# One decode-and-prefill layer on one core: all key products on VectorE, and the memory scan moved in front of the convolution

## What is computed

```python
h = rms_norm(x, norm1_w)
z = h @ w_in                       # conv b, c, x; q; k; v; memory q; three gates
y_conv = (zb * short_conv(zc * zx)) @ w_conv_out
q = partial_rope(rms_norm(q, q_norm_w)); k = partial_rope(rms_norm(k, k_norm_w))
# prompt: causal attention over its own 256 tokens
# sample b: over 2048 past tokens (16 pages of 128 rows) and its own
k_past = cache_k[page_table]       # per sample 16 pages, (128, 8 heads * 2 * 64)
s = einsum(q, k) * 64 ** -0.5      # differential attention: softmax 1 - lam * softmax 2
# prompt: memory keys and values from mem_prompt @ w_mem_kv, normed
# sample b: from cache_mem_k, cache_mem_v (256 tokens, 4 heads * 256)
qm = rms_norm(mq, mq_norm_w); s = einsum(qm, mem_k) * 256 ** -0.5
x = x + (sum_b sigmoid(gate_b) * y_b) @ w_o
x = x + peer_ffn(rms_norm(x, norm2_w))   # 8 heads, top 16 of 16384 experts per token
```

## Time and profile before

| | |
|---|---|
| profiled execution | 2749.54 us, span 2747.8 us |
| median of 3 runs | 2750.61 us (2749.42 to 2750.76) |
| TensorE busy | 2443.3 us (89%) |
| VectorE busy | 1431.9 us (52%) |
| ScalarE busy | 352.9 us (13%) |
| GpSimd busy | 1055.8 us (38%) |
| moved by DMA | 919.33 MB, mean 335 GB/s |
| key page scan (VectorE) | 116.24 to 485.8 us |
| memory projection (TensorE) | 446.96 to 575.4 us |
| gates and branches (TensorE) | 581.83 to about 1228 us |

### The profile page before, as it was taken

How to read it: one execution, slowest core, us unless ns; L and a number is a source line. 1 busy time by engine, 2 the same in 40 slices (tenths; PEclk the granted TensorE clock), 3 DMA queues, 4 the chain that set the end, 5 groups by cost and what they waited for, 6 DMA issues and landing times.

```text
span 2747.8 us, 27652 instructions
## 1 busy us (share of the span) xinstructions
PE 2443.3 (89%) x9109; PEld 1570.1 (57%) x9109; DVE 1431.9 (52%) x2306; ACT 352.9 (13%) x781; POOL 1055.8 (38%) x953
## 2 busy tenths in 40 slices
PE   9999998899999999999997777777999597777777
PEld 7888887778766678888884233332434142332333
DVE  3465566972322323002378877884554556554543
ACT  2111000012222211001112101111011011111110
POOL 1265566110222200000056555754544464445542
PEclk9999999999999999999999999998999899999999
DMA  7698999593799965447498999999999999999998
GB/s 225 225 343 311 323 345 333 203 343 123 280 353 352 355 215 187 159 149 235 138 369 344 422 418 417 416 418 422 422 413 422 412 408 418 419 421 418 416 421 370
DMA packets 305904, 919.33 MB, mean 335 GB/s; under 512 B 15738, under 2 KB 196050, under 8 KB 236756
## 3 DMA queue, kind: packets, MB, share of 16 engines
q0 software_dynamic: 122448, 725.64, 65.7%
q1 hardware_dynamic: 183332, 192.20, 21.4%
HBM read 909.08 MB, written 8.72 MB: 334 GB/s over the span
## 4 chain that ended last, share of the span: by engine, by line
PE 36%; DMA 24%; issue 13%; POOL 13%; DVE 11%; POOLq 2%; ACT 0%; DVEq 0%; SPq 0%; ACTq 0%
DMA sb_bregion<-in_peer_u_dram,sb_ring 14%; PE ps L788 13%; PE ps L800 6%; PE ps L694 4%; PE ps L1037 4%; DMA sb_mkv<-in_peer_u_dram,sb_ring 4%; DVE sb_bregion L1988 3%; POOL sb_ring L450 3%; POOL sb_mkv L450 3%; PE ps L888 2%; DMA sb_S<-in_peer_u_dram,sb_ring 2%; PE ps L778 2%; POOLq L441 2%; POOL sb_bregion L566 2%; POOL sb_wring L566 2%
## 5 line engine op out<-in xcount | busy, mean ns | idle before, releaser
L1037 PE MATMUL ps<-sb_wring,sb_ring 128*128 128x512 f32 x992 | 455.1, 608 | 86.7 <-DMA sb_wring<-in_peer_v_dram,sb_ring 86.6
L694 PE MATMUL ps<-sb_hT,sb_wring 128*128 128x264 f32 x1792 | 407.7, 388 | 3.4 <-DMA sb_wring<-in_w_in_dram 1.9
L1988 DVE CUSTOM_DVE_ANT_0 sb_bregion<-sb_bregion,sb_rows 128x2048 f32<-128x2048 f32 x128 | 293.5, 2293 | 217.2 <-DMA sb_bregion<-in_peer_u_dram,sb_ring 209.9
L1037 PEld LDWEIGHTS ps<-sb_wring,sb_ring 128*128 128x128 f32 x992 | 186.2, 194 | 354.4 <-issue 271.2
L694 PEld LDWEIGHTS ps<-sb_hT,sb_wring 128*128 128x128 f32 x1792 | 339.6, 191 | 62.2 <-issue 3.3
L788 PE MATMUL ps<-sb_hT,sb_wring 128*128 128x264 f32 x1536 | 368.2, 391 | 6.6 <-DMA sb_wring<-in_w_in_dram 5.1
L788 PEld LDWEIGHTS ps<-sb_hT,sb_wring 128*128 128x128 f32 x1536 | 289.2, 191 | 70.5 <-issue 16.4
L1037 PE MATMUL ps<-sb_oreg,sb_ring 128*128 128x512 f32 x496 | 236.1, 626 | 74.4 <-DMA sb_oreg<-in_peer_v_dram,sb_ring 52.0
L1037 PE MATMUL ps<-sb_hT,sb_ring 128*128 128x512 f32 x496 | 231.6, 614 | 53.6 <-DMA sb_hT<-in_peer_v_dram,sb_ring 47.5
L566 POOL DMA_INDIRECT sb_bregion<-in_peer_u_dram,sb_ring x132 | 185.7, 1407 | 226.1 <-DVEq L1376 194.5
L1037 PEld LDWEIGHTS ps<-sb_oreg,sb_ring 128*128 128x128 f32 x496 | 96.1, 200 | 213.5 <-issue 144.9
(11 more groups left out here) (376 smaller groups left out, 2785.1 us busy)
## 6 DMA issues: line engine op xcount, KB each, us to landing
sb_wring<-in_w_in_dram SPq DMA_DIRECT2D x52, 2048.0 KB, 13.0
sb_ring<-in_cache_k_dram POOLq DMA_DIRECT2D x64, 512.0 KB, 6.8
sb_mkv<-in_cache_k_dram POOLq DMA_DIRECT2D x64, 512.0 KB, 6.7
sb_mkv<-in_cache_v_dram POOLq DMA_DIRECT2D x48, 512.0 KB, 7.1
sb_rows<-in_cache_v_dram POOLq DMA_DIRECT2D x47, 512.0 KB, 7.2
sb_wring<-in_w_mem_kv_dram SPq DMA_DIRECT2D x8, 2048.0 KB, 11.7
sb_wring<-in_w_o_dram SPq DMA_DIRECT2D x8, 2048.0 KB, 8.1
sb_S<-in_cache_v_dram POOLq DMA_DIRECT2D x22, 512.0 KB, 6.8
```

Of the source, the lines that this page charges most:

```text
L694: last = mm(ps[:, (2 * r + c) % 4, 0:NT], wring[:, r, k, c * P:(c + 1) * P], rhs[:, k, :], start=(k == 0), stop=(k == KC - 1))
L1037: last = mm(ps[:, 4 * t + q, :], diag[:, k % 4, :], e_slots[v % ER][:, q * 512:(q + 1) * 512], start=False, stop=q_stop, skip_group_check= ...
L1988: st(V.tensor_tensor_reduce(out=u_slots[n % UR], in0=u_slots[n % UR], in1=h2, scale=1.0, scalar=0.0, op0=ALU.mult, op1=ALU.add, accum_out= ...
```

## The change

- `multiply_pages` and `kprod_ready` go. GpSimd only loads pages in the scan, in a loop of four turns with 8 groups each. VectorE multiplies all four pages of a group itself, into two product places in turn, and frees a page as soon as its product is made.
- The memory scan moves from behind the memory key norm to right behind the norms of the key and query rows. Its pages use the eight places of the key pages (`MEM_PAIR` picks pairs; tokens 0 and 1 use the four in `mkv` and are loaded before the norms, tokens 2 and 3 those in `ring4` after them), and each later pair is loaded two tokens ahead.
- ScalarE's memory copies wait for the end of the memory scan (2 + 16). `root(4)` moves in front of the last four convolution copies. The wait of ScalarE at the third gate chunk goes, as does GpSimd's wait for `sqrt_in`.
- The copy of the convolution state and the own maxima follow the memory key norm directly.
- The weights' blocks stay at 256 columns.

```diff
-        mem_pages = [ring4[:, n, :] for n in range(4)] + [conv_y[:, n * DC:(n + 1) * DC] for n in range(2)]
-        MEM_PAIR = [0, 1, 2, 0, 1, 2, 1, 2]
+        MEM_PAIR = [2, 3, 0, 1] * 2
...
-            load_pages(0, 0)
-            with st.loop(TS // 2 - 1, 16) as i:
+            with pool.Fori(0, TS // 2) as i:
                 for g in range(8):
-                    load_pages(i, g + 1)
-                    multiply_pages(i, g)
-            for g in range(8):
-                if g < 7:
-                    load_pages(TS // 2 - 1, g + 1)
-                multiply_pages(TS // 2 - 1, g)
+                    load_pages(i, g)
...
+            pool.wait_ge(s["kpage_used"], 8 + TS * PAGES)
+            load_memory(0)
+            load_memory(1)
             pool.wait_ge(s["q_ready"], 2)
             pool.dma_start(mq_dram, rows[0:TS, 2, 3 * DC:4 * DC]).then_inc(s["q_scratch"], 16)
             pool.wait_ge(s["q_scratch"], 32)
...
+            load_query(0)
+            load_query(1)
+            load_memory(2)
+            load_memory(3)
...
-            pool.wait_ge(s["sqrt_in"], 5)
-            load_memory(2)
             for b in range(2, TS):
                 pool.wait_ge(s["token_done"], 2 + TS + (b - 2) + 1)
                 load_query(b)
-                if b < 5:
-                    load_memory(b + 1)
-                elif b > 5:
-                    load_memory(b)
+                if b + 2 < TS:
+                    load_memory(b + 2)
...
-            conv_chunks(0, 6)
-
-            act.wait_ge(s["token_done"], 2 + TS)
+            conv_chunks(0, 5)
+            root(4, small[:, 3, 0:60])
+            conv_chunks(5, 1)
+
+            act.wait_ge(s["token_done"], 2 + 2 * TS)
...
-            root(4, small[:, 3, 0:60])
...
-                if q == 2:
-                    act.wait_ge(s["token_done"], 2 + TS + 4)
...
+                for r in range(4):
+                    dve.wait_ge(k_landed[4 * half + r], landed)
+                    if r >= 2:
+                        st.reach(k0 + r + 1)
+                    elif g:
+                        st.reach(k0 + r - 1)
+                    st.run(TT(prods[r % 2], slots[r], qb[:, par, :], ALU.mult))
+                    if r % 2:
+                        for p in (r - 1, r):
+                            st.reach(k0 + 2 * (r - 1) + p % 2 + 1)
+                            signal("kpage_used")
+                            st.run(RED(out(p), by_head(prods[p % 2]), X, ALU.add))
...
             signal("q_ready")
 
+            def score_memory(b):
...
+            for b in range(TS):
+                score_memory(b)
 
             dve.wait_ge(s["chunk_taken"], C_MEM + 4)
...
-            for b in range(TS):
-                score_memory(b)
-                if b == 4:
-                    dve.wait_ge(s["cs_full"], 1)
-                    st(CP(cs_rows[0:2 + TS, :].rearrange("p (a b) -> p a b", a=2), ps[0:2 + TS, 6:8, :]))
-                    signal("cs_rows")
-                if b == 5:
-                    own_maxima()
+            dve.wait_ge(s["cs_full"], 1)
+            st(CP(cs_rows[0:2 + TS, :].rearrange("p (a b) -> p a b", a=2), ps[0:2 + TS, 6:8, :]))
+            signal("cs_rows")
+            own_maxima()
```

More of the change, by code:

```diff
@@ L130, in build @@
         ring_flat = ring4[:, :, :].rearrange("p a b -> p (a b)")
-        conv_y = conv[:, 2 * BC:3 * BC, :].rearrange("p a b -> p (a b)")
-        mem_pages = [ring4[:, n, :] for n in range(4)] + [conv_y[:, n * DC:(n + 1) * DC] for n in range(2)]
-        MEM_PAIR = [0, 1, 2, 0, 1, 2, 1, 2]
+        MEM_PAIR = [2, 3, 0, 1] * 2
         scores = cflat[:, 0:3 * 2 * PH * NKEY].rearrange("p (t n) -> p t n", t=3)
@@ L209, in build @@
         names = """consts x_in x_in1 x_in2 x_factors x_clear xT_scaled mem_in cols_in st_in small_in lam_in rope_in pt_in x_ss xT_kept xT_back xT_full xT_taken
-            cols_full st_full st_taken chunk_full chunk_taken tr_full rows_taken kprod_ready
+            cols_full st_full st_taken chunk_full chunk_taken tr_full rows_taken
             scores_clear q_ready qk_stored q_scratch kpage_used token_done conv_ready cs_full cs_rows
@@ L442, in load_pages @@
                     pool.dma_start(kpages[4 * half + r], cache_k[ds(page * PAGE, PAGE), :]).then_inc(k_landed[4 * half + r], 16)
[L444 to L451, removed]
-            load_pages(0, 0)
-            with st.loop(TS // 2 - 1, 16) as i:
-                for g in range(8):
-                    load_pages(i, g + 1)
-                    multiply_pages(i, g)
-            for g in range(8):
-                if g < 7:
-                    load_pages(TS // 2 - 1, g + 1)
-                multiply_pages(TS // 2 - 1, g)
-            pool.wait_ge(s["q_ready"], 2)
-            pool.dma_start(mq_dram, rows[0:TS, 2, 3 * DC:4 * DC]).then_inc(s["q_scratch"], 16)
-            pool.wait_ge(s["q_scratch"], 32)
+            with pool.Fori(0, TS // 2) as i:
+                for g in range(8):
+                    load_pages(i, g)
             def load_query(b):
@@ L474, in load_memory @@
                     n = 2 * MEM_PAIR[b] + t
-                    pool.dma_start(mem_pages[n], cmem_k[b * NM + t * P:b * NM + (t + 1) * P, :]).then_inc(k_landed[n], 16)
-            for b in range(2):
-                load_query(b)
-                load_memory(b)
+                    pool.dma_start(kpages[n], cmem_k[b * NM + t * P:b * NM + (t + 1) * P, :]).then_inc(k_landed[n], 16)
+            pool.wait_ge(s["kpage_used"], 8 + TS * PAGES)
+            load_memory(0)
+            load_memory(1)
+            pool.wait_ge(s["q_ready"], 2)
+            pool.dma_start(mq_dram, rows[0:TS, 2, 3 * DC:4 * DC]).then_inc(s["q_scratch"], 16)
+            pool.wait_ge(s["q_scratch"], 32)
+            load_query(0)
+            load_query(1)
+            load_memory(2)
+            load_memory(3)
             for c, (po, so) in ((1, ("k_prompt", "k_sample")), (2, ("v_prompt", "v_sample"))):
@@ L1492, in score_group @@
                 k0 = st.k
[L1493 to L1510, removed]
+                for r in range(4):
[10 more added lines that the diff above has]
+                            st.run(RED(out(p), by_head(prods[p % 2]), X, ALU.add))
+            with st.loop(TS // 2, 8 * 8) as i:
                 for g in range(8):
@@ L1516, in _ @@
                     if g % 4 == 3:
+                        st.settle()
                         signal("token_done")
@@ L1522, in _ @@
             signal("q_ready")
+            def score_memory(b):
+                par, k0 = b % 2, st.k
+                dve.wait_ge(qb_landed[par], 64 + 16 * (b // 2 + 1))
+                for t in range(2):
+                    n = 2 * MEM_PAIR[b] + t
+                    dve.wait_ge(k_landed[n], 256 + 16 * (MEM_PAIR[:b].count(MEM_PAIR[b]) + 1))
+                    st.run(TT(prods[t], kpages[n], qb[:, par, :], ALU.mult))
+                for t in range(2):
+                    st.reach(k0 + t + 1)
+                    st.run(RED(Sm_f[:, b * 8 + t * 4:b * 8 + t * 4 + 4], prods[t].rearrange("p (g w) -> p g w", w=MD), X, ALU.add))
+                st.settle()
+                signal("token_done")
+            for b in range(TS):
+                score_memory(b)
             dve.wait_ge(s["chunk_taken"], C_MEM + 4)
```

## The result

| | before | changed |
|---|---|---|
| median | 2750.69 us (runs beside the changed kernel) | 2796.81 us (4 runs, 2793.99 to 2801.47) |
| ratio | 1 | 1.0174, 95% interval 1.0161 to 1.0186 |
| profiled execution | 2749.54 us, span 2747.80 | 2798.33 us, span 2796.6 |
| page scan ends | 485.8 us | 414.5 us |
| last weight wait of the convolution over | 357.8 us | 382.6 us |

The account below looks back on a forecast made before the run. TensorE's gate matmuls were taken to set the end, their start following ScalarE's permission to write the memory projection. That comes 21.5 us later, less 11.0 returned: +10.5 us, 2760.0 profiled, 2761.1 against the median; range 2747 to 2790.

Parts of the forecast that it names:

- (1): Key page scan with all products on VectorE: 303 us, bounds 296 and 344, ending at 419.2 instead of 485.8.
- rival B: The DMA engines bound the page scan: 344 us at 349 GB/s, +52 us, half way +31; chance 0.13.
- The 380 GB/s over 19 us: Rate seen with both DMA queues full, used for the page scan's 300 us of DMA and against the skill's 358.
- (2): Key and query norms after the scan: unchanged 32.3 us, 419.2 to 451.5; ScalarE's earlier root free or 1 to 2 us.
- (3): Memory scan moved ahead of the convolution: 56 us, bounds 50 and 65, making R 507.5, 21.5 us later.
- R: Time at which ScalarE may start writing the memory projection: 486.0 before, 507.5 predicted; the kernel's end moves with it.
- (4): Gate stage start: weight waits of 3.09 and 5.07 us go, first 32 matmuls 2.8 us shorter; 11.0 us returned.
- (5): Convolution (16 us), own scores and page maxima (23 us) follow R free, while TensorE needs 86 us for 12 chunks.
- A: Two scans in a row outweigh what GpSimd's share cost: -0.5 to +27 us; chance 0.50.
- C: Code loading stops VectorE at its scan loop's back edges: +36 us, or +23 with one hole a turn; chance 0.13.
- D: Not slower: DMA engines keep up, scan 296 us, memory scan 50, R 494.5, -2.5 us; chance 0.18.
- E: Faster by over 0.2%: scan 290.6 us, instructions back to back, memory scan 49.7, R 488.8, -8 us; chance 0.06.

Follow-up runs that it names:

- e7: Changed kernel with QKV and convolution weight blocks read as 16 KB instead of 1 KB runs, from wrong rows, so other numbers are computed: 2757.91 us, ratio 1.0034.
- e1: Changed kernel with root(4) on ScalarE after 12 instead of 20 convolution copies: 2787.02 us, ratio 1.0135.
- e2: Kernel before with only all key products moved to VectorE; memory scan, root(4) and ScalarE's wait stay: 2786.74 us, ratio 1.0133.
- e5: e2 with four page places handed out at the start instead of eight: 2758.08 us, ratio 1.0035.
- e9: e2 with V's and the convolution's weights fetched in 2 KB instead of 1 KB runs: 2754.31 us, ratio 1.0018.
- e10: Changed kernel with V's and the convolution's weights in 2 KB instead of 1 KB runs: 2776.80 us (2768.59 to 2786.56), ratio 1.0112.

## Why the prediction was wrong

(1) *The scan*: its end was right, in part by luck. The norms begin at 414.92 against 419.2. But the sum took 303 us from the DMA engines, and what set the time was VectorE's own pace, its 296 us: starts 1.13 us apart, 14.7 us of waits for pages, 11.1 of them before the first. The pages were not the ones to wait, and rival B fell. The sum had put the weights' 142 GB/s first and given the pages the rest, 71.3 / (0.380 - 0.142). It is the other way about: the pages kept 70.03 MB / 294 us = 238 GB/s in every kernel with five places or more, and the weights in 1 KB runs got what was left.

The prediction's rows could have said so in engine time. By the earlier trace rows a MB of pages took 0.507 x 370 x 16 / 70.12 = 42.8 us of one DMA engine, a MB of weights in 1 KB runs 0.431 x 370 x 16 / 52.43 = 48.7. Pages at 0.238 MB a us (VectorE's pace in the prediction, 71.3 MB in 296 us, asks for 0.241) and weights at 0.142 need 0.238 x 42.8 + 0.142 x 48.7 = 17.1 engines, and there are 16. The changed kernel shows nearly the same prices, 0.642 x 294 x 16 / 70.03 = 43.1 and 0.340 x 294 x 16 / 33.56 = 47.7. In e7, with 16 KB runs, a MB of weights took 39.5 and of pages 41.3: 15.4 engines, which fits. The weights bore the whole shortage: 41.94 - 33.56 = 8.4 MB are four blocks, 4 x 14.5 = 58 us of TensorE, and the memory projection began 498.7 - 447.0 = 52 us late.

The 358 GB/s that the Trainium skill gives for a core ("DMA: Bandwidth & Descriptors", section "Where 436 GB/s comes from") is close to the 346 to 359 that held here while 1 KB and 4 KB packets kept the engines 97% busy or more. The 380 GB/s over 19 us, by which it had been set aside, could not be kept up over 294 us with 1 KB runs, but was with 16 KB runs: 381. And the page of the kernel before shows 408 to 422 GB/s in every slice from about 1510 to 2680 us. So it is no fixed limit in this kernel, and in the window of the scan the rate rose with the length of the runs. Its use in the prediction was on the scan, which didn't get slower.

(2) *The root, "free, or 1 or 2 us of TensorE's reserve"*: false, 42.59 us. An instruction that VectorE waits for was placed behind 20 copies whose times TensorE sets; it is free only while TensorE is on time.

(3) *The memory scan*: right. The norms ended 17.8 us after the root (489.25), and the memory scan took 57.7 us against 56, with 8.76 idle before the first product, 7.41 before token 2, 0.2 to 1.8 between the others. Token 2 began 25.3 us after the norms where the sum had 26.5; no run shows the 1 us in it for a load's latency by itself. "TensorE may lose 10 to 20 us to slower weights, that is what hides them" is the step that failed. The prediction's own numbers left it 507.5 - 476.5 = 31 us; it lost some 52, by which TensorE was late itself (e1: 2787.0 with the root out of the way) and, through (2), R as well: 547.0 instead of 507.5. The difference of 39.5 is -4.3 (scan) + 42.6 (root, less the 0.4 that e1 shows it to take anyway) + 1.7 (memory scan). In the changed kernel TensorE fills its banks at 541.8, just before R and 34 us after the R that was predicted. The prediction had named this case, TensorE full only after R, among what would make it wrong, and had given it neither a price nor a chance.

(4) *What comes back*: right. The gate stage starts without a wait, its first 32 matmuls in 7.39 us. R is 61.0 us later than before and the span 48.8 us longer, so 12.2 us came back against 11.0. A new wait came before it, 12.66 us for memory weights at 525.33, in the same stretch as the memory pages and the stores of k and v; here it ended before R and cost nothing.

(5) *Free*: right; own maxima and the convolution show nowhere in the chain.

Rivals: A's sizes were right but for the weights, and e7, where these are in time, measured 2757.9. C fell: the changed kernel's VectorE stands 0.9 to 1.2 us at its back edges. D had the scan right, and died of the same step as A; E would have needed a scan without any gap.

## What to carry to other kernels

Before a queue is made faster, add up the engine time that all queues need at their full rates, each with its own cost per MB by the length of its runs, and ask who bears the shortage: here the stream of 1 KB runs, which fed the engine that sets the end. On the products alone, a throttle (four places instead of eight, e2 to e5) gave 29 us back, 2 KB runs (e2 to e9) 32, and both 48. And an instruction that another engine waits for belongs where its own engine is early, not behind copies that a third engine sets.

## What the hardware showed unasked

- The length of weight runs, at the same bytes and with pages loading at full rate, moved the landing of a 2 MB block from 18.8 us (1 KB) over 15.3 (e10, mostly 2 KB) to 10.3 (e7, 16 KB), and what both queues moved from 353 over 368 to 381 GB/s. Why the page queue keeps its rate against the weight queue was not tested.
- What a MB costs in time of one DMA engine barely moved from kernel to kernel while the engines were 94% busy or more: 47.5 to 48.7 us for weights in 1 KB runs and 41.3 to 43.5 for the pages, whose runs are 4 KB, where one kernel (e7) gave 39.5 for 16 KB.
- GpSimd's holes at the back edge went with the shorter loop. Before, its loads at 214.48 and 311.06 come after 9.98 and 9.44 us without a cause on record (324 instructions a turn, my count); the changed kernel has 265 a turn, and its first edge, in front of the load of the third token's query (L435), shows none:

```profile
173.68 0.53 POOL L440 DMA_DIRECT2D sb_mkv<-in_cache_k_dram  x1 [0.78 <-issue]
174.73 0.53 POOL L435 DMA_DIRECT2D sb_oreg<-q_rows_scratch  x1 [0.52 <-issue]
176.91 0.53 POOL L440 DMA_DIRECT2D sb_ring<-in_cache_k_dram  x1 [1.65 <-DVEq L1356]
```

One hole of 4.63 us at 350.81, inside a turn, has no explanation. Nor do the holes of the kernel before: rival C took them for code loading, but by the reading that it gives, a turn of 265 instructions should show them as well, and shows none.
